# A mixer of retention, gated and convolution branches: convolution panels first, another rule for the taps, level operands scaled ahead of the masked copy

## The reference, cut to what matters

```python
rq, rk, rv, rg, gq, gf, gi, gg, ca, cb, gates = jnp.split(h @ w_in, bounds, axis=-1)
o = _retention(_rope(rq), _rope(rk) * 128 ** -0.5, rv)        # 4 heads of 128
u_a = norm(o) * ret_norm_g * silu(rg)
f = lb + (1 - lb) * sigmoid(gf)
o = _hgrn2(silu(gq), log(f), 1 - f, gi)                       # 4 heads, S_t = diag(f_t) S_{t-1} + k_t v_t^T
u_b = rms(o) * hgrn_norm_g * silu(gg)
u = _causal_dwconv(ca * sigmoid(cb), conv_w, conv_b)          # 512 channels, 31 taps
u_c = silu(_layer_norm(u, conv_ln_g, conv_ln_b))
y = sum(sigmoid(gates[:, :, b]) * (u_x @ w_branch[b]) for b, u_x in enumerate((u_a, u_b, u_c)))
return y @ w_out
```

## Time and profile before

| | |
|---|---|
| time, median of 3 runs | 3551.8 us (3549.53 to 3557.51) |
| the profiled execution | 3556.7 us |
| its span, first to last instruction | 3554.9 us |
| mean granted clock of PE | 0.983 |
| PE busy | 3351.4 us, 94% |
| DVE busy | 2145.4 us, 60% |
| ACT busy | 1285.2 us, 36% |
| the two mixers' part with heads and taps | about 1600 to 1965 us and 2605 to 2971 us |

### The profile page before, as it was taken

How to read it: one execution, slowest core, us unless ns; L and a number is a source line. 1 busy time by engine, 2 the same in 40 slices (tenths; PEclk the granted TensorE clock), 3 DMA queues, 4 the chain that set the end, 5 groups by cost and what they waited for, 6 DMA issues and landing times. The chain is left out here.

```text
span 3554.9 us, 38889 instructions
## 1 busy us (share of the span) xinstructions
PE 3351.4 (94%) x15296; PEld 2673.0 (75%) x15296; DVE 2145.4 (60%) x2741; ACT 1285.2 (36%) x1652; POOL 603.7 (17%) x488
## 2 busy tenths in 40 slices
PE   7899999999999999999988998999899979989997
PEld 5677788886677788877767886888677758868886
DVE  7854566448644666458885346555568864265545
ACT  4664322235663322233222325333433232243333
POOL 2122222121212212201001122010200002120002
PEclk9999999999999999999999999999999989999999
DMA  3122455222223554232111232222222112322221
GB/s 123 45 62 82 177 198 194 107 95 64 50 72 140 186 190 160 88 104 71 68 51 48 89 103 95 95 95 89 77 71 71 66 36 77 107 72 95 96 102 63
DMA packets 72181, 344.44 MB, mean 97 GB/s; under 512 B 25152, under 2 KB 26048, under 8 KB 35648
## 3 DMA queue, kind: packets, MB, share of 16 engines
q1 hardware_dynamic: 70416, 339.12, 27.7%
q0 software_dynamic: 576, 2.33, 0.2%
q10 hardware_dynamic: 1008, 0.51, 0.0%
HBM read 340.51 MB, written 2.10 MB: 96 GB/s over the span
## 5 line engine op out<-in xcount | busy, mean ns | idle before, releaser
L855 PE MATMUL bank<-Hhi_b,whi_b 128*128 128x512 f32 x2976 | 1224.6, 411 | 73.5 <-ACT Hhi_b L1957 22.1
L856 PE MATMUL bank<-Hhi_b,wlo_b 128*128 128x512 f32 x2976 | 1173.5, 394 | 0.0
L862 PE MATMUL bank<-Hlo_b,whi_b 128*128 128x512 f32 x2976 | 1163.8, 395 | 1.0 <-DVE Hlo_b L2252 0.8
L833 DVE TENSOR_TENSOR wlo_b<-raw_b,whi_b 128x2048 fp32r<-128x2048 f32 (+2 forms) x290 | 624.0, 2152 | 555.2 <-ACT whi_b L827 555.0
L855 PEld LDWEIGHTS bank<-Hhi_b,whi_b 128*128 128x128 f32 x2976 | 568.5, 191 | 224.5 <-issue 40.8
L856 PEld LDWEIGHTS bank<-Hhi_b,wlo_b 128*128 128x128 f32 x2976 | 568.7, 191 | 124.7 <-issue 13.8
L862 PEld LDWEIGHTS bank<-Hlo_b,whi_b 128*128 128x128 f32 x2976 | 565.1, 190 | 126.5 <-DVE Hlo_b L2252 5.5
L827 ACT ACTIVATE whi_b<-raw_b 128x2048 fp32r<-128x2048 f32 (+2 forms) x290 | 511.4, 1764 | 354.6 <-PE bank L862 351.4
L855 PE MATMUL bank<-Uhi_b,whi_b 128*128 128x512 f32 x1024 | 406.6, 397 | 0.0
L856 PE MATMUL bank<-Uhi_b,wlo_b 128*128 128x512 f32 x1024 | 399.0, 390 | 0.0
L862 PE MATMUL bank<-Ulo_b,whi_b 128*128 128x512 f32 x1024 | 385.5, 390 | 0.0
(11 more groups left out here) (249 smaller groups left out, 3468.3 us busy)
## 6 DMA issues: line engine op xcount, KB each, us to landing
raw_b<-in_w SPq DMA_DIRECT2D x234, 1024.0 KB, 4.9
ada_b<-in_wada SPq DMA_DIRECT2D x48, 1024.0 KB, 7.0
raw_b<-in_w SPq DMA_DIRECT2D x40, 512.0 KB, 3.6
raw_b<-in_w SPq DMA_DIRECT2D x16, 768.0 KB, 4.3
rel_b<-in_rel SPq DMA_DIRECT2D x128, 24.0 KB, 2.4
X_keep<-in_x SPq DMA_DIRECT2D x4, 512.0 KB, 8.9
decay_b<-in_decay POOLq DMA_DIRECT2D x2, 1024.0 KB, 6.8
out<-X_keep SPq DMA_DIRECT2D x8, 256.0 KB, 2.0
```

Of the source, the lines that this page charges most:

```text
L833: self.nc.vector.tensor_tensor(self.wlo[n % RAW_SLOTS][:, 0:words], self.raw[n % RAW_SLOTS][:, 0:words], self.whi[n % HI_SLOTS][:, 0:words ...
L855: self.nc.tensor.matmul(out, whi[:, k, cols], xhi, start=(k == 0), stop=False)
L856: self.nc.tensor.matmul(out, wlo[:, k, cols], xhi, start=False, stop=False)
L862: mm = self.nc.tensor.matmul(out, whi[:, k, cols], xlo, start=False, stop=(k == nk - 1))
```

## The change

1. `mixer_panels` puts the convolution's panels at 0, 1, 6 and 9 and the retention heads at 2 to 5, 7, 8, 10 and 11. Gated heads 0 and 1 have panels 12 to 15, then come a gate and a projection panel of branch 0 (16, 17), head 2 (18, 19), again gate and projection (20, 21), head 3 (22, 23), and gates and projections of branch 1 (24 to 27). Panel 28, the first gate panel of branch 2, joins `ahead`.
2. `gap` takes the number of taps from `taps_beside`: two behind a piece of a retention or convolution panel, three behind one of a gate or projection panel, none behind one of a gated head's panels, except one for head 3.
3. On DVE a level first multiplies the halves of `RQ` and `RK` and then does the masked copy; level 0 multiplies by `FT` ahead of the product with the identity. The cross items do likewise. The instructions are the same ones.

```diff
--- before.py
+++ after.py
@@ -450,9 +450,19 @@
 
     ret = [head("rq", "rk", "rv", "rg", i) for i in range(4)]
     hgrn = [head("gq", "gf", "gi", "gg", i) for i in range(4)]
-    ahead = ret[0] + ret[1] + conv(0) + ret[2] + conv(1) + ret[3] + conv(2) + hgrn[0] + conv(3) + hgrn[1]
-    ahead += hgrn[2] + mixed(0, 0, (0,)) + hgrn[3] + mixed(0, 0, (1,)) + mixed(1, 0)
-    return ahead, mixed(2, 0) + mixed(0, 1) + mixed(1, 1) + mixed(2, 1)
+    ahead = conv(0) + conv(1) + ret[0] + ret[1] + conv(2) + ret[2] + conv(3) + ret[3]
+    ahead += hgrn[0] + hgrn[1] + mixed(0, 0, (0,)) + hgrn[2] + mixed(0, 0, (1,)) + hgrn[3] + mixed(1, 0)
+    last, *rest = mixed(2, 0) + mixed(0, 1) + mixed(1, 1) + mixed(2, 1)
+    return ahead + [last], rest
+
+
+def taps_beside(kind, a):
+
+    if kind != "z":
+        return 3
+    if a[0] in ("gq", "gi"):
+        return int(a[1] == 3)
+    return 2
 
 
 MIX_FROM = (0, 8, 4)
@@ -576,10 +586,10 @@
                 s.temp("st", 2, ("st", l, "cfin", item[2]))
             s.add(*item)
 
-        def gap():
+        def gap(taps):
             if chain:
                 run(chain.pop(0))
-            for _ in range(2):
+            for _ in range(taps):
                 if conv:
                     run(conv.pop(0))
 
@@ -626,7 +636,7 @@
         for i, (kind, a, b) in enumerate(ahead + behind):
             if i == len(ahead):
                 while chain or conv:
-                    gap()
+                    gap(1)
             if kind == "z":
                 h = a[1]
                 if a[0] == "rq":
@@ -658,7 +668,7 @@
                 for piece in s.lazy_product(n, nk, 256, cols, rhs, then):
                     piece()
                     if i < len(ahead):
-                        gap()
+                        gap(taps_beside(kind, a))
             n += 1
         out_end, ffn_end = n + 4, n + 4 + FFN_PANELS
         n = out_stages(s, n, l, lambda c: ln_column(s, out_end, l, "mix", c), halfway=lambda: ln_half(s, l, "mix"))
@@ -2143,16 +2153,28 @@
                 dve.wait_ge(*after(*job))
                 if kind == "level" and i == 0:
 
+                    dve.wait_ge(*after("FT", l, b, h))
+                    nv.tensor_tensor(q, q, buf(("FT", l, b, h)), ALU.mult).then_inc(*mark("dve", ("lv", l, h, 1)))
                     reuse(dve, ("at", l, b, h))
                     v = "p (t n) -> p t n"
                     nv.tensor_tensor(AT[:, 0:SEQ].rearrange(v, t=TT), out.rearrange(v, t=TT),
                                      keep.ident[:].unsqueeze(1).to_broadcast([P, TT, P]), ALU.mult)\
                         .then_inc(*mark("dve", ("al", l, h, 0), ("free", job)))
-                    dve.wait_ge(*after("FT", l, b, h))
-                    nv.tensor_tensor(q, q, buf(("FT", l, b, h)), ALU.mult).then_inc(*mark("dve", ("lv", l, h, 1)))
                     continue
+                L = LEVELS[i - 1] if kind == "level" else (128, 256)[i]
+                if L < 256:
+
+                    tot = totals(l, h, L).rearrange("p (b two) -> p b two", two=2)
+                    nb = SEQ // (2 * L)
+                    q4, k4 = halves(q, L), halves(kk, L)
+                    if L > 1:
+                        dve.wait_ge(*after("tl", l, h, L))
+                    dve.wait_ge(*after("lv", l, h, L))
+                    nv.tensor_tensor(q4[:, :, 1], q4[:, :, 1], tot[:, :, 0:1].to_broadcast([P, nb, L]), ALU.mult)\
+                        .then_inc(*mark("dve", ("lq", l, h, L)))
+                    nv.tensor_tensor(k4[:, :, 0], k4[:, :, 0], tot[:, :, 1:2].to_broadcast([P, nb, L]), ALU.mult)\
+                        .then_inc(*mark("dve", ("lv", l, h, 2 * L)))
                 if kind == "level":
-                    L = LEVELS[i - 1]
                     if h == 0 and i == 1:
                         dve.wait_ge(table_landed, 32 * (l + 1))
                     dve.wait_ge(*after("al", l, h, i - 1))
@@ -2162,25 +2184,11 @@
                                        out.rearrange(v, t=TT))\
                         .then_inc(*mark("dve", ("al", l, h, i), ("free", job)))
                 else:
-                    L = (128, 256)[i]
                     n, to = ((256, 512), (512, 768))[i]
                     names = [("ax", l, h, i), ("free", job)]
                     if i == 1:
                         names += [("free", ("FT", l, b, h))]
                     nv.tensor_copy(AT[:, to:to + n], out[:, 0:n]).then_inc(*mark("dve", *names))
-                    if i == 1:
-                        continue
-
-                tot = totals(l, h, L).rearrange("p (b two) -> p b two", two=2)
-                nb = SEQ // (2 * L)
-                q4, k4 = halves(q, L), halves(kk, L)
-                if L > 1:
-                    dve.wait_ge(*after("tl", l, h, L))
-                dve.wait_ge(*after("lv", l, h, L))
-                nv.tensor_tensor(q4[:, :, 1], q4[:, :, 1], tot[:, :, 0:1].to_broadcast([P, nb, L]), ALU.mult)\
-                    .then_inc(*mark("dve", ("lq", l, h, L)))
-                nv.tensor_tensor(k4[:, :, 0], k4[:, :, 0], tot[:, :, 1:2].to_broadcast([P, nb, L]), ALU.mult)\
-                    .then_inc(*mark("dve", ("lv", l, h, 2 * L)))
                 if 2 * L in tl_at:
                     nv.tensor_tensor(totals(l, h, 2 * L), tot[:, :, 0], tot[:, :, 1], ALU.mult)\
                         .then_inc(*mark("dve", ("tl", l, h, 2 * L)))
```

## The result

The changed kernel is slower: 3572.9 us (median of 5 runs, 3567.1 to 3577.9) beside 3557.3 for the kernel before in the same session; ratio 1.0047, 95% interval 1.0033 to 1.0061. That is some 16 us where I had said 11, and the time lies 11 above the one forecast, inside the range. The profiled executions differ by less, 3567.1 against 3556.7; each program varies by some 10 us, and the profiled run of after is the fastest of its five.

A forecast was written before the change was run, and what follows sets the result against it. PE, busy for 94% of the span, was taken to bound the kernel. Terms of +6.5 us in layer 0 and +5 in layer 1, about +11 on a median of 3551.8, gave 3562 us, range 3540 to 3580.

The forecast's parts named there:

- (g): Norm of gated head 3, now right before branch 2's projection panel: new wait of 6.4 us, with clock +9.2 per layer.
- (c): Norm of gated head 0 to level 1 of head 1: wait of 7.0 us, with clock +0.6 per layer.
- (d): Norm of gated head 1 to head 2: wait of 5.5 us for the panel, with clock -1.0 per layer.
- Rival 1: The heads run free of taps and waits (c) and (d) shrink to about 3 us each: 3539 us, chance 0.25.
- Rival 2: Losses cancel: (g) right, but (e) gives 3 us more per layer and small waits 2 more: 3553, chance 0.30.
- (e): Convolution's norm between the levels of gated head 2: -1 us in layer 0, -2.5 in layer 1, sizes least sure.
- Rival 3: Scaling order buys nothing and three taps make (c) and (d) 2 us worse each: 3570 us, chance 0.10.
- 0 by itself: Scaling ahead of the masked copy: 0.6 us at 28 places, counted only within other waits, otherwise worth 0.
- 0 to +0.5: Retention heads, head 1 newly with taps beside its norm: about 13 us of PE work against 12.5, 0 to +0.5.
- (f): Norm of gated head 2 to head 3: wait of 3.1 us and 1.5 of clock, -2.1 per layer.
- The table load: ACT's load in the norm's chain, taken as 1.28 us; by the skill's 2.66, new wait 7.8, sum 2.8 higher.
- (b): End of retention to gated head 0: 7.2 us with clock against 6.6 before, +0.6 per layer.

The follow-up runs named there:

- recip: The changed kernel with a plain copy of the root in place of its reciprocal in the gated heads' norms: 3545.4 us, ratio 0.9959.
- lvl_only: The kernel before with only DVE's scaling moved ahead of the masked copy: 3546.1 us, ratio 0.9968.
- no_y7: The changed kernel, with branch 2's first projection panel reading head 2's output again in place of head 3's: 3568.8 us, ratio 1.0035.
- early_no_y7: no_y7 with an edit meant to reorder ACT that left every engine's instruction order the same: ratio 1.0026.
- quiet_u_lvl: lvl_only with ACT rounding the next panel before a gated head's output, and taps moved from gated norm gaps to retention score blocks: 3518.3 us, ratio 0.9885.

## Why the prediction was right or wrong

**The sign and the mechanism were right.** Term (g) stood as written: a wait of 6.22 and 6.21 for 6.4, at the matmul with `Uhi`, released by `Ulo`. The same holds for the norm's chain behind four waits (recip), for (c) with 7.1 and 7.5 for 7.0, for (d) with 5.0 for 5.5, for the squares of retention head 3 with 1.9 for 2.0, and for the cadence of head 0's levels, 1754.66 - 1751.04 = 3.62 for 3.6. Rival 1 fails: (c) and (d) add up to 12 us and more, without their clock, as large as before. Rival 2 fails on size; (e) did give a little more, but not 5 us a layer in all. (By its own working, "3.4 less" from +0.4 is 2 below the -1 taken and not 3; its time would have been 3555.) Rival 3 fails in both halves: the scaling order is worth 11 us.

**"0 by itself" was the step on the scaling.** I counted its 0.6 only at (c). In lvl_only it was worth 11 us by the runs and 10 by the waits, since most level waits are the end of a serial path and get shorter by the full 0.6. In the sum this error was hidden, I think, because I had taken the waits after the change by their whole length and not as a difference.

**"0 to +0.5" for the retention heads** was too small: +1.3 and +1.2, and at head 1 alone +1.8 in both layers. The rows on DVE behind the norm of head 0 show what was missing; first before, then after:

```profile
1603.70 1.78 DVE L2094 TENSOR_TENSOR RQ_b<-t_b,t_b 128x512 f32<-128x512 f32 x1 [2.71 <-POOL t_b L1833]
1606.31 0.69 DVE L2094 TENSOR_TENSOR RK_b<-t_b,t_b 128x512 f32<-128x512 f32 x1
```

```profile
1619.26 2.67 DVE L2069 SCALAR_TENSOR_TENSOR acc_b<-Up_b,vec_b,acc_b 128x512 f32<-128x512 f32 x2
1621.85 0.68 DVE L2099 TENSOR_TENSOR t_b<-bank,sin_b 128x512 f32<-128x512 f32 x1
1623.12 1.77 DVE L2104 TENSOR_TENSOR RQ_b<-t_b,t_b 128x512 f32<-128x512 f32 x1 [0.59 <-POOL t_b L1843]
1624.81 1.53 DVE L2069 SCALAR_TENSOR_TENSOR acc_b<-Up_b,vec_b,acc_b 128x512 f32<-128x512 f32 x2
...
1627.04 0.69 DVE L2104 TENSOR_TENSOR RK_b<-t_b,t_b 128x512 f32<-128x512 f32 x1
```

```profile
1620.09 1.29 POOL L954 TENSOR_TENSOR Ulo_b<-ON_b,Uhi_b 128x512 fp32r<-128x512 f32 x1 [49.69 <-ACT Uhi_b L951]
1621.33 3.01 POOL L1843 TENSOR_TENSOR t_b<-qf_b,cos_b 128x512 f32<-128x512 f32 x2
```

From the start of `RQ` to the end of `RK` are 3.3 us before and 4.6 after: a second pair of taps stands between them, where I had counted one pair in all. The first pair lies where DVE had waited 2.71 for POOL before and costs only 0.5. From the norm's last product on DVE (which ended at 1600.40 before and 1619.34 after) to the end of `RK` it is 6.6 and 8.4 us, and the difference is the 1.8 by which the wait grew. My 12.5 was too short for another reason also: two taps last 2.67 while POOL makes `Ulo` and 1.53 when it is idle, and the addition into `RQ`, 0.69 otherwise, takes 1.77 beside POOL's product (as it did before). I had used this at (d) and not here. The Trainium skill (GPSIMD Engine Reference, Specifications) says that GpSimd shares its SBUF interfaces with VectorE and contends with instructions that have two SBUF inputs; both of these have two, and the trace agrees.

**(f), "-2.1", failed by its sign**: +0.4 of waits. I let ACT go from `Uhi` straight to the next panel, as the earlier trace rows show it. In the new order a gate's sigmoid lies between them:

```profile
1922.55 0.63 ACT L951 ACTIVATE Uhi_b<-ON_b 128x512 fp32r<-128x512 f32 x1 [4.22 <-DVE ON_b L2146]
1923.20 1.28 ACT L918 ACT_TABLE_LOAD   x1
1924.49 0.60 ACT L918 ACTIVATE sg_b<-bank 128x512 f32<-128x512 f32 x1
1924.98 2.85 ACT L837 ACTIVATE whi_b<-raw_b 128x2048 fp32r<-128x2048 f32 x2
```

1.28 + 0.60 less the overlap is 1.8 us later, and the wait is 4.7 for my 3.1. **(e)** went the other way: 6.5 us of waits in layer 0, not 9.9. In the sum the two partly cancel, and that is luck. How much of (e) is the change isn't settled either: one of its waits is 3.27 in no_y7 and 4.86 in its repeat early_no_y7.

**The table load.** The root starts at the end of the 1.28 us load here too (1.30 from start to start in the rows of no_y7), and (g) is 6.2, not 7.8. It isn't that ACT was idle before: the load at 1923.20 in the last rows starts 0.02 us after the end of `Uhi`, and the sigmoid 1.29 after the load's start. The 2.66 us that the Trainium skill gives for a switch (ScalarE: Activation LUTs, What ACT_TABLE_LOAD costs) do not show up on this path; the measurement decides.

**Size of the sum.** By the profiled pair my +11 met +10.3 us; by the medians it is +16, with an interval of 12 to 22. That the profiled pair came so near is in part luck: after's profiled run was the fastest of its five, and the mixer's first panel gave it 3.9 us which at least in part are chance. Of the 10.9 us between forecast and result 4.6 are this, 0.8 is my rounding down to 3562, and 5.5 are the base: 3551.8 was the median of three runs, with two more it is 3557.3, and later sessions gave 3556.7 to 3563.1 for the same kernel.

**What I did not see at all** is that (g) had a second holder (no_y7). My rule that ACT goes in order was in the text, as a reason for the panels at (d) and (f), and I did not apply it to the panel behind (g).

## What to carry to other kernels

A norm's serial chain costs PE what it is longer than PE's next independent work, and from there on each us of the chain is a us of PE (recip); so look at what each in-order queue holds right behind it. Here the next panel's split and the taps were stuck behind it on ACT and DVE, though neither needed it, and to move them away gave 30 us (lvl_only to quiet_u_lvl), where the change had moved the chain itself to the place with the least cover. When a wait is removed, the next one on the same stretch may stand 15 matmuls later: take both holders away before calling a term wrong. And price a reordering that shortens a serial path at every wait that ends on that path, not at zero.

## What the runs showed of the hardware that I had not expected

A DVE instruction with two SBUF inputs that meets a running POOL instruction is not slowed by a factor, it is held until that one ends. The second tap at 1619.26 ends at 1621.93, 0.55 us behind POOL's `Ulo` (1621.38), and the addition at 1624.89, 0.55 behind POOL's second product (1624.34). In the whole trace of after all 54 such instructions of 128x512 that took over 0.8 us (up to 1.90, for 0.68 to 0.75) ended 0.55 us behind the end of a POOL instruction, to within 0.01. One that started 0.05 us or more ahead of POOL's kept its 0.68 to 0.75, and so did four that started in the last 0.07 us of POOL's. Products of the same size with an input from a PSUM bank took 0.69 in the mean beside POOL (109 of them) and 0.70 without (369).

And waits at one place differ between two traces of the same order of instructions (no_y7 and early_no_y7, layer 0): 1.71 and 4.56 us at the mixer's first panel, 1.83 and 3.44 at level 1 of head 0, 3.27 and 4.86 beside the convolution's norm. That is as much as several of the terms above, (b) and (e) among them: a single pair of traces does not settle a few us. The waits behind the gated heads' norms agree within 0.02 there.
